# Input projection of a hybrid decoder step: token-major blocks in pairs of 512 columns, channel blocks moved ahead, more places for weights

## What is computed

```python
xn = rms_norm(x, norm1_w)                    # (1152, 1024)
q, k, v, z, xBC, dt, gA, gS = split(xn @ W_in)     # 768,768,768, 1024, 1536, 16, 1024, 1024 columns
xc = silu(conv_b + sum(xBC_padded[:, t:t + L] * conv_w[t] for t in range(4)))
dt = softplus(dt + dt_bias)
```

## Time and profile before

| | |
|---|---|
| runs, median (lowest to highest) | 2130.43 us (2129.21 to 2132.47), 3 runs |
| profiled execution | 2131.87 us |
| its span in the profile | 2130.1 us |
| the projection | first 450 us of the span |
| mean granted TensorE clock | 0.934 |

### The profile page before, as it was taken

The page is one execution under the profiler, slowest core; times in us unless marked ns, Lnnn a source line. Parts: engine busy times, 40 slices in busy tenths (PEclk is TensorE's granted clock), DMA queues, the critical chain, the costliest instruction groups (busy, mean ns, idle before and its releaser), DMA issues. The chain is left out here.

```text
span 2130.1 us, 29088 instructions
## 1 busy us (share of the span) xinstructions
PE 1876.4 (88%) x11611; PEld 1657.1 (78%) x11611; DVE 1215.6 (57%) x1278; ACT 816.6 (38%) x1173; POOL 396.4 (19%) x386
## 2 busy tenths in 40 slices
PE   7999999989996999888876998975999999999960
PEld 7899999978885887677745998764788888888850
DVE  4333333326655320476635545227988888888846
ACT  5211111114332331222224222123777777777732
POOL 0000000035441221222240000003721111111103
PEclk9999999989997999999977999986999999999985
DMA  7355555344435965644335334327999999999947
GB/s 233 131 167 171 170 171 174 123 156 123 141 95 142 225 178 155 209 159 164 125 126 182 118 100 136 136 89 285 361 425 410 404 406 405 404 404 406 402 193 266
DMA packets 202441, 472.37 MB, mean 222 GB/s; under 512 B 34551, under 2 KB 160279, under 8 KB 189250
## 3 DMA queue, kind: packets, MB, share of 16 engines
q1 hardware_dynamic: 140418, 321.84, 42.9%
q0 software_dynamic: 16688, 73.60, 10.3%
q10 hardware_dynamic: 45200, 75.06, 9.5%
HBM read 375.53 MB, written 121.93 MB: 234 GB/s over the span
## 5 line engine op out<-in xcount | busy, mean ns | idle before, releaser
L2884 DVE TENSOR_TENSOR k_w_lo<-expert_raw,k_w_hi 128x4096 fp32r<-128x4096 f32 x96 | 424.2, 4421 | 70.9 <-ACT k_w_hi L2828 70.9
L2828 ACT CAST k_w_hi<-expert_raw 128x4096 fp32r<-128x4096 f32 x96 | 348.4, 3632 | 106.5 <-PE k_pu L74 64.1
L72 PE MATMUL a_acc<-a_w_hi,x_hi 128*128 128x256 f32 x648 | 186.5, 288 | 0.3 <-DVE x_lo L231 0.3
L73 PE MATMUL a_acc<-a_w_lo,x_hi 128*128 128x256 f32 x648 | 184.6, 285 | 0.0
L74 PE MATMUL a_acc<-a_w_hi,x_lo 128*128 128x256 f32 x648 | 184.6, 285 | 0.0
L72 PEld LDWEIGHTS a_acc<-a_w_hi,x_hi 128*128 128x128 f32 x648 | 125.7, 194 | 0.7 <-DVE x_lo L231 0.5
L73 PEld LDWEIGHTS a_acc<-a_w_lo,x_hi 128*128 128x128 f32 x648 | 125.7, 194 | 0.0
L74 PEld LDWEIGHTS a_acc<-a_w_hi,x_lo 128*128 128x128 f32 x648 | 125.6, 194 | 0.0
L72 PE MATMUL k_po<-k_w_hi,k_h_hi 128*128 128x512 f32 x256 | 102.4, 400 | 10.6 <-DVE k_h_lo L2905 10.6
L72 PE MATMUL k_pu<-k_w_hi,k_x_hi 128*128 128x512 f32 x256 | 104.7, 409 | 7.5 <-DVE k_w_lo L2884 7.5
L72 PE MATMUL k_pg<-k_w_hi,k_x_hi 128*128 128x512 f32 x256 | 102.4, 400 | 2.5 <-DVE k_x_lo L2889 2.5
(11 more groups left out here) (484 smaller groups left out, 4798.8 us busy)
## 6 DMA issues: line engine op xcount, KB each, us to landing
expert_raw<-in_w_expert_gate SPq DMA_DIRECT2D x32, 2048.0 KB, 10.3
expert_raw<-in_w_expert_up SPq DMA_DIRECT2D x32, 2048.0 KB, 12.2
expert_raw<-in_w_expert_down SPq DMA_DIRECT2D x32, 2048.0 KB, 11.6
m_T<-in_cache_kv_w SPq DMA_DIRECT2D x72, 256.0 KB, 4.3
scratch_o_moe<-k_out ACTq DMA_DIRECT2D x32, 512.0 KB, 11.5
a_w<-in_w_in SPq DMA_DIRECT2D x15, 1024.0 KB, 7.2
scratch_u_tm<-m_T ACTq DMA_DIRECT2D x81, 128.0 KB, 2.2
scratch_o_moe<-e_zeros POOLq DMA_DIRECT2D x8, 1024.0 KB
```

The lines of the kernel that those rows point to most:

```text
L72: nc.tensor.matmul(out, one_pass(a_hi), one_pass(b_hi), start=(i == 0), stop=False)
L73: nc.tensor.matmul(out, one_pass(a_hi), one_pass(b_lo), start=False, stop=False)
L2828: nc.scalar.copy(one_pass(w_hi[:, kind, :]), raw[:, c % NRAW, :]).then_inc(s_hi, 1)
L2884: nc.vector.tensor_tensor(one_pass(w_lo[:, kind, :]), raw[:, c % NRAW, :], w_hi[:, kind, :], ALU.subtract).then_inc(s_lo, 1)
```

## The change

Token-major blocks t1 to t8 are done in pairs, "p": one unit streams 512 columns into a whole accumulator. The order becomes t0, d, x0, x1, x2, p1, x3, p3, x4, p5, x5, p7. Divided weights get a third place: pairs use the first two side by side, x blocks from x2 on use the third. Raw weights get four places, one of their own for the first two blocks and three that lie over the input's buffers (usable once all nine tiles are turned). `xt` moves to a tile of a later phase, and stores of token-major results go through three places of 512 columns. The turns of an x step now also happen inside a following x step. Cut to its core:

```diff
-PROJECT = ([("t", 0), ("d", 0), ("t", 1)] + [x for p in range(N_XB) for x in (("x", p), ("t", p + 2))]
-           + [("t", n) for n in range(N_XB + 2, N_TM)])
+PROJECT = [("t", 0), ("d", 0), ("x", 0), ("x", 1), ("x", 2), ("p", 1), ("x", 3), ("p", 3), ("x", 4), ("p", 5), ("x", 5), ("p", 7)]
-BLOCK_STEPS = [i for i, (kind, _) in enumerate(PROJECT) if kind != "d"]
+BLOCK_STEPS = [i for i, (kind, _) in enumerate(PROJECT) for _ in range({"d": 0, "p": 2}.get(kind, 1))]
+BLOCK_SLOTS = [0, 1, 0, 2, 0, 1, 2, 0, 1, 2, 0, 1, 2, 0, 1]
+BLOCK_RAW = [0, 0] + [1 + b % 3 for b in range(2, 15)]
...
-        NACC, NST = 4, 6
+        NACC, NST = 4, 3
...
                 def load_w(b):
-                    if b >= 2:
-                        sp.wait_ge(s_split, b - 1)
-                    kind, n = PROJECT[BLOCK_STEPS[b]]
-                    c = block_cols(kind, n)
-                    sp.dma_start(tm(w[:, b % 2, :]), w_in[:, :, c:c + WCOL]).then_inc(s_w[b % 2], 16)
+                    a = last_in(BLOCK_RAW, b)
+                    if a is not None:
+                        sp.wait_ge(s_split, a + 1)
+                    elif BLOCK_RAW[b] > 0:
+                        sp.wait_ge(s_turned, TILES)
+                    c = block_cols(b)
+                    sp.dma_start(raw_place(b), w_in[:, :, c:c + WCOL]).then_inc(s_w[BLOCK_RAW[b]], 16)
+
+                def load_history(p):
+                    for u in range(2):
+                        n = 2 * p + u
+                        if n >= 2:
+                            sp.wait_ge(s_sums, n - 1)
+                        sp.dma_start(xs[:, u, :, 0:HIST], T["state_conv"][n * 128:(n + 1) * 128, :, :]).then_inc(s_hist[u], 16)
...
-                load_w(1)
                 for n in range(3, TILES):
                     load_x(n)
+                load_history(0)
+                load_w(1)
                 for b in range(2, len(BLOCK_STEPS)):
                     load_w(b)
                     kind, p = PROJECT[BLOCK_STEPS[b]]
                     if kind == "x":
-                        for u in range(2):
...
+                        load_history(p)
...
                 for i, (kind, p) in enumerate(PROJECT):
-                    if kind == "t" and i > 0 and moved < NB:
+                    if i >= 2 and moved < NB:
                         pool.wait_ge(s_split, block_of(i))
                         move_cache(moved)
...
                 def split_block(b):
-                    dve.wait_ge(s_w[b % 2], (b // 2 + 1) * 16)
-                    if b >= 2:
-                        dve.wait_ge(s_acc, FIRST_UNIT[BLOCK_STEPS[b - 2] + 1])
...
+                    a = last_in(BLOCK_SLOTS, b)
+                    dve.wait_ge(s_w[BLOCK_RAW[b]], (BLOCK_RAW[:b].count(BLOCK_RAW[b]) + 1) * 16)
+                    if a is not None:
+                        dve.wait_ge(s_acc, FIRST_UNIT[BLOCK_STEPS[a] + 1])
...
                 for i, (kind, p) in enumerate(PROJECT):
                     if i == 0 or kind == "d":
                         continue
-                    if block_of(i) + 1 < len(BLOCK_STEPS):
-                        split_block(block_of(i) + 1)
+                    for b in blocks(i + 1):
+                        split_block(b)
                     if i == 2:
                         step_sizes()
                         dve.wait_ge(s_zero, 1)
-                    if kind == "x":
-                        convolve(2 * p)
-                        convolve(2 * p + 1)
-                    if after_x(i):
-                        take_turned(2 * PROJECT[i - 1][1])
-                        take_turned(2 * PROJECT[i - 1][1] + 1)
+                    for u in range(2):
+                        if after_x(i):
+                            take_turned(2 * PROJECT[i - 1][1] + u)
+                        if kind == "x":
+                            convolve(2 * p + u)
...
                     elif kind == "x":
-                        take_x(i, 2 * p)
-                        take_x(i, 2 * p + 1)
+                        if i == 2:
+                            step_sizes_log()
+                        for u in range(2):
+                            if after_x(i):
+                                silu(2 * PROJECT[i - 1][1] + u)
+                            take_x(i, 2 * p + u)
...
-                    if kind == "t":
+                    if kind == "p":
                         for m in range(TILES):
                             unit_tm(i, m)
-                            if i == 2 and m == 4:
-                                turn_step_sizes()
-                            if after_x(i) and m in (2, 6):
+                            if after_x(i) and m in (1, 4):
                                 turn_convolved(2 * PROJECT[i - 1][1] + m // 4)
                     else:
                         for u in range(2):
                             for c in range(len(CHUNKS)):
                                 unit_cm(i, u, c)
+                            if i == 2 and u == 0:
+                                turn_step_sizes()
+                            if after_x(i):
+                                turn_convolved(2 * PROJECT[i - 1][1] + u)
```

More of the change, by code:

```diff
@@ L104, in phase_project @@
         x_in, xn = (early[:, i * 3 * D:(i + 1) * 3 * D].rearrange("p (u d) -> p u d", u=3) for i in range(2))
-        w, w_hi, w_lo = (sb(n, [128, 2, KT * WCOL]) for n in ("w", "w_hi", "w_lo"))
+        w = sb("w", [128, KT * WCOL])
+        w_hi, w_lo = (sb(n, [128, KT, 2, WCOL]) for n in ("w_hi", "w_lo"))
+        third_hi, third_lo = (sb(n, [128, KT, WCOL]) for n in ("third_hi", "third_lo"))
         ident, eps = T["eye"], sb("eps", [128, 1])
@@ L124, in phase_project @@
         s_const, s_cw, s_eps, s_row, s_row_bc = sm("const"), sm("cw"), sm("eps"), sm("rowt"), sm("rowbc")
-        s_x, s_w = [sm(f"x{u}") for u in range(3)], [sm(f"w{u}") for u in range(2)]
+        s_x, s_w = [sm(f"x{u}") for u in range(3)], [sm(f"w{u}") for u in range(4)]
         s_std, s_xn, s_turned, s_xhi, s_xlo = (sm(n) for n in ("std", "xn", "turned", "xhi", "xlo"))
@@ L131, in phase_project, with raw_place, place, blocks @@
         s_zero, s_xr, s_sums, s_xc, s_pe, s_ev, s_xt = (sm(n) for n in ("zero", "xr", "sums", "xc", "pe", "ev", "xt"))
-        n_tiles_stored = N_TM * TILES
-        def block_cols(kind, n):
-            return {"t": n * WCOL, "x": XOFF + n * WCOL}[kind]
+        n_tiles_stored = (1 + (N_TM - 1) // 2) * TILES
+        def raw_place(b):
+            i = BLOCK_RAW[b] - 1
+            return tm(early[:, i * KT * WCOL:(i + 1) * KT * WCOL] if i >= 0 else w)
+        def place(x, s):
+            if s == 2:
+                return (third_hi, third_lo)[x][:, :, :]
+            return (w_hi, w_lo)[x][:, :, s, :]
+        def blocks(i):
+            return [b for b, j in enumerate(BLOCK_STEPS) if j == i]
+        def last_in(slots, b):
+            return max([a for a in range(b) if slots[a] == slots[b]], default=None)
+        def block_cols(b):
+            kind, n = PROJECT[BLOCK_STEPS[b]]
+            return XOFF + n * WCOL if kind == "x" else (n + b - BLOCK_STEPS.index(BLOCK_STEPS[b])) * WCOL
         def tm(w):
@@ L339, in store_tm @@
                 def store_tm(i, n, m):
-                    q, j = FIRST_UNIT[i] + m, n * TILES + m
+                    q, j = FIRST_UNIT[i] + m, (n + 1) // 2 * TILES + m
+                    width = 2 * WCOL if n else WCOL
                     act.wait_ge(s_acc, q + 1)
@@ L343, in store_tm @@
                         act.wait_ge(s_st[j % NST], j // NST * 16)
-                    nc.scalar.copy(o_tm[:, j % NST, :], acc[q % NACC][:, 0:WCOL]).then_inc(s_out, 1)
+                    nc.scalar.copy(o_tm[:, j % NST, 0:width], acc[q % NACC][:, 0:width]).then_inc(s_out, 1)
                     act.wait_ge(s_out, q + 1)
-                    act.dma_start(T["u_tm"][m * 128:(m + 1) * 128, n * WCOL:(n + 1) * WCOL], o_tm[:, j % NST, :]
+                    act.dma_start(T["u_tm"][m * 128:(m + 1) * 128, n * WCOL:n * WCOL + width], o_tm[:, j % NST, 0:width]
                                   ).then_inc(s_st[j % NST], 16)
@@ L410, in _ @@
                         step_sizes_in(i)
-                    elif kind == "t" and i > 0:
+                    elif kind == "p":
                         for m in range(TILES):
                             store_tm(i, p, m)
[L414 to L417, removed]
+                            if after_x(i) and m in (0, 2):
+                                silu(2 * PROJECT[i - 1][1] + m // 2)
                     elif kind == "x":
-                        take_x(i, 2 * p)
-                        take_x(i, 2 * p + 1)
+                        if i == 2:
[4 more added lines that the diff above has]
+                            take_x(i, 2 * p + u)
                 for i in range(NST):
@@ L441, in unit_tm @@
                 def unit_tm(i, m):
-                    slot, q = block_of(i) % 2, FIRST_UNIT[i] + m
-                    hi, lo = tm(w_hi[:, slot, :]), tm(w_lo[:, slot, :])
```

(18 more changed lines are left out.)

12 lines of the change are left out of this document (6 added, 6 removed).

## The result

The changed kernel took 2143.32 us (median of 6 runs, 2139.6 to 2153.46), the kernel before 2129.82 (6 runs, 2127.62 to 2133.85). The ratio is 1.0061 [1.0044, 1.0078]: slower by 0.6%, or 13 us. The forecast was 2139, slower, in a range of 2130 to 2150. The profiled execution took 2144.6 us, 12.7 more than the one before, and its span is 2142.8 us.

A forecast was written before the change was run, and what follows sets the result against it. TensorE was taken to bound the projection; −11.8 − 3.0 + 4.7 + 13.6 + 4.4 + 0.7 = +8.6 us gave 2140.5 us for the profiled execution and a median of 2139, range 2130 to 2150.

The forecast's parts named there:

- The sign and the place: Whole kernel: slower, 2139 us, with the change confined to the projection and TensorE stalling in x1 and x2.
- The pairs: Token-major blocks: 864 matmuls of 512 columns replace 1728 of 256, saving 0.0136 us each, 11.8 us.
- The third rival: Pair steps: wide matmuls at 0.2331 us apart gain only 6.0 us; total +14.4, 2145; chance 0.08.
- the other price: Pair steps: an isolated matmul costs N/2.4 + 2.5 ns, so all pairs save about 2.2 us; chance at most 0.02.
- The first turns of the pair steps: Four pair steps: VectorE is free when the first convolved column is transposed, gaining 4 × 0.74 = 3.0 us.
- x1: First column turn in x1: TensorE waits for VectorE, which divides late-loaded weights first; 7.0 us lost instead of 2.3, +4.7.
- x2: First column turn in x2: two late loads, slowed by a cache move, and two divisions come first; +13.6 us.
- The second rival: x2: the cache move does not hold up the weight loads; x2 costs 9.9, total +4.9, 2135; chance 0.24.
- the first: x1 and x2: the turns find VectorE free, so no stalls; total −14.1, 2116; chance 0.12.
- The fourth: x2: both loads land at their high ends, +19.5 there; total +14.5, 2145; chance 0.10.
- The clock: After the stalls in x1 and x2: TensorE returns at its lower clock, +2.2 us each, 4.4.
- The tail: End of the projection: the last, larger copy and store are not hidden, 0.2 plus 0.5, +0.7 us.

The follow-up runs named there:

- experiment 1: Changed kernel with SyncE loading the next step's weights before the history loads of a channel block; 2120.4 us, ratio 0.9949 to the kernel before.
- experiment 2: Changed kernel with VectorE in x1 and x2 taking the first turned column and convolving before dividing weights; 2126.67 us, ratio 0.9972 to the kernel before.
- experiment 4: Changed kernel with each pair unit's 512 columns multiplied as two runs of 256; 2154.04 us, ratio 1.011 to the kernel before.
- experiment 3: Changed kernel without the cache move in x2, each later move one step later; 2135.51 us, ratio 1.001 to the kernel before.
- experiment 6: Changed kernel with weight loads before history loads, one division before each x1 and x2 turn, first cache move later; 2113.12 us, ratio 0.9909 to the kernel before.

## Why the prediction was right, and where it was off

- **The sign and the place: right.** The projection is bound by TensorE, the pairs shorten its work, and two late turns give back more. Experiments 1 and 2 show the chain link by link: either order mended, and the loss is gone.
- **The pairs: right.** −11.8 forecast, −11.6 in the profile, some 10 in experiment 4's runs. The third rival (0.2331 us, a gain of 6.0) does not hold. Nor does the other price, of 2.2 us: the isolated gap of the Trainium skill, "TensorE: Matmul & The Clock Gate", "Back-to-back issue gap", gave it, and the spacings of 0.1200 and 0.2277 us are both 13 to 14 ns over N/2.4 (N columns at 2.4 GHz), not 2.5.
- **The first turns of the pair steps: right,** −3.0 and −2.7.
- **x1: right in its mechanism,** +4.7 and +3.8. The load took 6.1 us, not 7.2, within the bounds.
- **x2: the mis-sized term,** +13.6 and +17.3. The term that was too small is the landing of the first load, which the prediction put "just after the move". The end of the move was right (17.7 us after x2's start, 17.4 measured), but the load came 23.4 after it, not 18.2: SyncE's packets had hardly moved, and the history load and the weights took 5.9 us more. That is 5.2 too little. A second error took 1.7 back: I let the second load land 5.2 after the first and then divided for 3.5, 8.7 in all; it was there in time, and the two divisions ran on end in 7.0. The second rival, that the move has no part, is ruled out by experiment 3; the first falls with both stalls. The fourth (+19.5) was nearer to x2's 17.3 than the forecast.
- **The clock: right.** 2.2 each, 4.4; measured 2.0 and 2.4.
- **The tail: right,** 0.7 and 0.9. Neither the places over the inputs nor the casts in strips (1.22 and 1.23 us, as in the earlier trace rows) cost anything.
- **The sum:** 8.6 forecast, 13.9 between the two profiles. Of the 5.3, x2 is 3.7, the start 1.5 (within the spread of the profiles), the rest small terms.

The landing in x2 was drawn from the earlier trace rows, whose load went out 0.3 us ahead of its move. By 67 us, as the move's large packets set in, all but 0.21 MB of that load was through; the kernel before from 67 to 77 us, columns as in experiment 3:

```profile
q1 hardware_dynamic: 224, 0.21, 8.4%
```

The load of x2, issued 5 us into its move, had no such start.

What stays open: whether the new order of the steps, channel blocks first, brings anything by itself. No run has it without the pairs.

## What to carry to other kernels

When steps are put back to back, look at each in-order queue for what stands ahead of the step's loads: a 12 KB load that waits for a late result delays every megabyte behind it, and reordering those issues alone was worth some 24 us here (1.0063 to 0.9949). Before a large copy is placed, ask which load will be in flight beside it, and compare the sizes of their packets, not only their bytes. And order the work of a helping engine by who waits for it: the copy that TensorE needs now goes ahead of the division that it needs a block later.

## What was not expected of the hardware

- **The clock fell after 1.89 us of idle.** In experiment 1 TensorE did eight transposes at 132.25, waited 1.89 us, did the rest of the turn and went on. Granted clock by stretch of TensorE's work (length, busy, clock, DMA share, GB/s):

```profile
134.00:136.00 2.00, 0.82 (x4) 0.83 0.46 164
136.00:138.00 2.00, 2.00 (x8) 0.50 0.68 145
```

0.50 is the lower level, 1.2 GHz, and the matmuls of 384 columns went at 0.32 us instead of 0.17 meanwhile, which cost the 1.6 us. The idle of up to 1.1 us in the turns of the kernel before cost no clock: it is 1.00 from 128 to 140 us, around the first of these turns, and the 48 matmuls of 256 columns behind it took 5.84 us, as behind the turns with 0.4 us of idle.
- **A load issued into a running cache move makes little headway until it ends.** 15.6 us instead of 5.9 for 1 MB, 13.7 instead of 3.7 for 512 KB, 13.2 instead of 2.4 for 12 KB: the engines are not shared by bytes, as the packets of experiment 3 show.
- **The kernel before pays for this too,** behind idle time of TensorE at its start that I had not looked at, as the change does not touch it. An estimate is 5 us: its step sizes' units begin at 57.50, those of experiment 6 at 52.22. No run has the kernel before with its first move put off.
